# Expert tokens in 32 chunks of 64 rows on both column halves of the PE array, instead of 24 chunks of 128 rows

## The reference, cut to what matters

```
x (544, 1024) = the normed rows
group  = argmax of x @ w_rg (4 groups); 2 best of the 4 experts in that group by x @ w_re
gate   = softmax over the two, times the group's probability
hid    = silu(x @ w1[e]) * (x @ w3[e])        w1, w3: 16 experts of (1024, 256)
y     += gate * hid @ w2[e]                   w2:     16 experts of (256, 1024)
```

## Time and profile before

| | |
|---|---|
| median of 3 runs | 1552.7 us (1549.16 to 1556.25) |
| the profiled execution's own time | 1555.62 us |
| its span in the profile | 1553.6 us |
| mean granted TensorE clock | 0.902 of full speed |
| TensorE matmul busy | 82% of the span |
| bytes moved by DMA | 304 MB, mean 196 GB/s |

### The profile page before, as it was taken

The page is one execution under the profiler, slowest core; times in us unless marked ns, Lnnn a source line. Parts: engine busy times, 40 slices in busy tenths (PEclk is TensorE's granted clock), DMA queues, the critical chain, the costliest instruction groups (busy, mean ns, idle before and its releaser), DMA issues.

```text
span 1553.6 us, 20055 instructions
## 1 busy us (share of the span) xinstructions
PE 1268.4 (82%) x6991; PEld 828.4 (53%) x6991; DVE 451.1 (29%) x1106; ACT 296.7 (19%) x613; POOL 160.9 (10%) x229
## 2 busy tenths in 40 slices
PE   3699999656699999957888888874995799999990
PEld 2377776433477777744555555553644444444440
DVE  4200000654212223223444443433445111111116
ACT  2200001322122122112222222211210111111112
POOL 0000000400111112200000000000000121111110
PEclk9899999777799999977898898877997799999995
DMA  8733332259522221079887888657001999999934
GB/s 309 263 108 110 111 108 100 81 180 332 187 81 63 88 77 56 12 271 313 281 274 251 266 286 291 234 199 259 26 31 36 336 334 318 309 313 331 312 122 172
DMA packets 152741, 304.23 MB, mean 196 GB/s; under 512 B 16014, under 2 KB 79271, under 8 KB 150176
## 3 DMA queue, kind: packets, MB, share of 16 engines
q1 hardware_dynamic: 143264, 281.55, 53.9%
q0 software_dynamic: 9408, 21.82, 3.8%
HBM read 283.37 MB, written 50.00 MB: 215 GB/s over the span
## 4 chain that ended last, share of the span: by engine, by line
PE 75%; DVE 10%; issue 4%; DMA 4%; SPq 4%; ACT 2%; another core or an unknown queue 1%; POOL 0%; DVEq 0%; POOLq 0%; ACTq 0%
PE psum L841 64%; PE psum L1124 6%; DVE arena L1720 3%; DMA wring<-in_w_mod 2%; PE psum L1163 2%; PE psum L1388 1%; DVE wring L1728 1%; SPq L628 1%; DVE hT L2300 1%; PE psum L1052 1%; PE psum L970 1%; DVE wring L1720 1%; DVE arena L1728 1%; DVE xT L2091 1%
## 5 line engine op out<-in xcount | busy, mean ns | idle before, releaser
L841 PE MATMUL psum<-hT,wring 128*128 128x272 f32 x1280 | 303.9, 396 | 8.3 <-ACT hT L1445 8.3
L841 PEld LDWEIGHTS psum<-hT,wring 128*128 128x128 f32 x1280 | 241.2, 191 | 68.8 <-issue 20.8
L841 PE MATMUL psum<-arena 128*8 128x128 f32 (+6 forms) x1488 | 207.6, 338 | 6.6 <-DVE arena L1720 3.5
L841 PE MATMUL psum<-wring,hT 128*128 128x512 f32 x384 | 173.0, 604 | 17.5 <-DVE hT L2300 15.4
L841 PEld LDWEIGHTS psum<-arena 128*8 128x8 f32 (+5 forms) x1488 | 109.9, 119 | 92.7 <-issue 78.3
L841 PE MATMUL psum<-wring,arena 128*8 128x128 f32 (+3 forms) x1008 | 118.2, 411 | 19.6 <-DMA wring<-in_w_mod 14.0
L841 PEld LDWEIGHTS psum<-wring,hT 128*128 128x128 f32 x384 | 71.8, 192 | 104.8 <-issue 101.8
L841 PEld LDWEIGHTS psum<-wring,arena 128*8 128x8 f32 (+3 forms) x1008 | 51.9, 111 | 74.2 <-issue 60.4
L841 PE MATMUL psum<-arena,small 128*128 128x256 f32 (+8 forms) x162 | 51.5, 442 | 39.7 <-DVE arena L1720 27.7
L1124 PE MATMUL psum<-small,arena 128*128 128x128 f32 x392 | 65.3, 322 | 20.8 <-DMA arena<-in_cache_kv 13.1
L779 POOL TENSOR_SCALAR wring<-wring,arena 128x384 f32<-128x384 f32 (+6 forms) x32 | 45.7, 1427 | 292.0 <-DVE arena L1939 292.0
(11 more groups left out here) (236 smaller groups left out, 1207.7 us busy)
## 6 DMA issues: line engine op xcount, KB each, us to landing
wring<-in_w SPq DMA_DIRECT2D x48, 1024.0 KB, 11.2
arena<-in_cache_kv SPq DMA_DIRECT2D x128, 320.0 KB, 3.5
wring<-in_w_mod SPq DMA_DIRECT2D x12, 2048.0 KB, 13.4
arena<-in_w SPq DMA_DIRECT2D x24, 1024.0 KB, 5.0
xT<-in_cache_kv SPq DMA_DIRECT2D x64, 320.0 KB, 3.5
wring<-in_cache_kv SPq DMA_DIRECT2D x64, 320.0 KB, 3.6
out_dil_sample<-in_cache_dil SPq DMA_DIRECT2D x8, 2044.0 KB, 37.0
wring<-in_w_in SPq DMA_DIRECT2D x6, 2048.0 KB, 11.8
```

The lines of the kernel that those rows point to most:

```text
L841: return T.matmul(out, lhsT, rhs, start=start, stop=stop, **k)
```

## The change

```
-CHUNKS = NEXP + (TOP * TOK - NEXP) // P
+CROWS = 64
+OVER = 16
+CHUNKS = NEXP + OVER
+WSLOTS = 4
...
+        OVER_AT = [n // 2 if n % 2 == 0 else OVER - 1 - n // 2 for n in range(OVER)]
...
+            def base_weights(e):
+                slot = 2 * e % WSLOTS
+                if e >= 2:
+                    sp.wait_ge(sem("h_mm"), 2 * (e - 2) + 1)
+                for n, name in enumerate(("w1", "w3")):
+                    sp.dma_start(w13_at[slot][:, n, :], I[name][0, e].rearrange("(p k) f -> p (k f)", p=P)
+                                 ).then_inc(sem(f"ld_e{slot}"), 16)
+                if e >= 2:
+                    sp.wait_ge(sem("y_mm"), 2 * (e - 2) + 1)
+                sp.dma_start(w2_at[slot], I["w2"][0, e].rearrange("(k p) f -> p k f", p=P)
+                             ).then_inc(sem(f"ld_e{slot}"), 16)
+            sp.wait_ge(sem("gate_mm"), 3 * GATES)
+            base_weights(0)
...                                   (the stores of h_d, as before)
-            sp.wait_ge(*done_at("exp_id"))
...
+            for e in range(1, NEXP):
+                base_weights(e)
...
             def scatter(c):
-                pool.wait_ge(sem("yc_evA"), c + 1)
-                pool.wait_ge(sem("yc_evD"), c + 1)
+                pool.wait_ge(sem("yc_ev"), c + 1)
                 settle()
                 pool.indirect_dma_start(
-                    out=y_d, out_offset=bass.IndirectOffsetOnAxis(ap=row_i[:, c:c + 1], axis=0),
+                    out=y_d.rearrange("t (a d) -> (t a) d", a=2),
+                    out_offset=bass.IndirectOffsetOnAxis(ap=row_i[:, c:c + 1], axis=0),
...
+            def over_weights(c):
+                slot, j = c % WSLOTS, OVER_AT[c // 2]
+                if c >= WSLOTS:
+                    pool.wait_ge(sem("h_mm"), c - WSLOTS + 1)
+                    pool.wait_ge(sem("y_mm"), c - WSLOTS + 1)
+                    settle()
+                for n, name in enumerate(("w1", "w3")):
+                    pool.indirect_dma_start(out=w13_at[slot][:, n, :], ...
+                for n in range(2):
+                    pool.indirect_dma_start(out=w2_at[slot][:, n, :], ...
             settle()
-            for c in range(CHUNKS + RING):
-                if c < CHUNKS:
-                    gather(c)
-                if c >= RING:
-                    scatter(c - RING)
+            for c in range(RING):
+                gather(c)
+            over_weights(1)
+            over_weights(3)
+            for c in range(CHUNKS):
+                scatter(c)
+                if c + RING < CHUNKS:
+                    gather(c + RING)
+                if c % 2 and c + WSLOTS < CHUNKS:
+                    over_weights(c + WSLOTS)
...
+            def turn_rows(c):                                  # TensorE
+                pe.wait_ge(sem(f"ld_g{c % RING}"), 16 * (c // RING + 1))
+                if c >= 2:
+                    pe.wait_ge(sem("xg_ev"), c - 1)
                 for k in range(KD):
+                    last = T.transpose(banks[c % 2][:, CROWS * k:CROWS * k + CROWS],
+                                       xrow[0:CROWS, c % RING, 128 * k:128 * k + 128], ident[0:CROWS, 0:CROWS])
+            def hidden(c):
...
                 for k in range(KD):
+                    for side in range(2):
+                        f0 = DE * k + P * side
+                        last = mm(banks[2 + c % 2][CROWS * side:CROWS * side + CROWS, 0:256],
+                                  xg[:, c % RING, CROWS * k:CROWS * k + CROWS], w13_at[slot][:, :, f0:f0 + P], ...
+            def outputs(c):
+                pe.wait_ge(sem("hidT_ev"), c + 1)
+                if c >= 2:
+                    pe.wait_ge(sem("yc_ev"), c - 1)
                 for k in range(2):
+                    for side in range(2):
+                        last = mm(banks[5 + c % 2][CROWS * side:CROWS * side + CROWS, :],
+                                  hidT[:, c % RING, CROWS * k:CROWS * k + CROWS],
+                                  w2_at[c % WSLOTS][:, k, 512 * side:512 * side + 512], ...
+            turn_rows(0)
+            turn_rows(1)
+            for c in range(CHUNKS):
+                hidden(c)
+                if c:
+                    outputs(c - 1)
+                if c + 2 < CHUNKS:
+                    turn_rows(c + 2)
+                turn_hidden(c)
+            outputs(CHUNKS - 1)
...
+            def outputs_out(c):                                # VectorE
+                dve.wait_ge(sem("y_mm"), c + 1)
+                if c >= RING:
+                    dve.wait_ge(sem(f"st_yc{c % RING}"), 16 * (c // RING))
+                V.tensor_copy(ychunk[:, c % RING, :], banks[5 + c % 2]).then_inc(sem("yc_ev"), 1)
```

More of the change, by code:

```diff
@@ L643, in _ @@
             sp.wait_ge(sem("row_t"), 5)
-            sp.wait_ge(*done_at("exp_id"))
[L646 to L671, removed]
+            for e in range(1, NEXP):
+                base_weights(e)
             for s in range(RING):
-                sp.wait_ge(sem(f"st_yc{s}"), 16 * (CHUNKS // RING))
+                sp.wait_ge(sem(f"st_yc{s}"), 16 * len(range(s, CHUNKS, RING)))
             for i in range(5):
@@ L1401, in turn_hidden @@
-            def turn_hidden(i, c0, slot):
-                pe.wait_ge(sem("hid_ready"), i * RING + (c0 + 1))
-                if c0:
-                    pe.wait_ge(sem("hidT_ev"), i * RING + c0)
-                for k in range(2):
-                    last = T.transpose(banks[5][:, 128 * k:128 * k + 128], hidr[:, slot, 128 * k:128 * k + 128], ident)
-                last.then_inc(sem("hid_t"), 1)
-            def outputs(i, c0, slot, before=True):
-                pe.wait_ge(sem("hidT_ev"), i * RING + (c0 + 1))
-                pe.wait_ge(sem(f"ld_e{slot}"), i * 16 + 16 * (c0 // RING + 1))
-                for half in range(2):
-                    if before:
-                        pe.wait_ge(sem("yc_evD" if half else "yc_evA"), i * RING + c0)
-                    for k in range(2):
-                        last = mm(banks[6 + half], hidT[:, slot, 128 * k:128 * k + 128],
-                                  wdown[:, slot, 1024 * k + 512 * half:1024 * k + 512 * half + 512], k == 0, k == 1)
-                    last.then_inc(sem("y_mm"), 1)
@@ L1421, in _ @@
-            turn_rows(0, 0, 0)
-            hidden(0, 0, 0)
-            turn_rows(0, 1, 1)
-            turn_hidden(0, 0, 0)
-            with pe.Fori(0, CHUNKS // RING - 1) as i:
-                for c0 in range(1, 1 + RING):
-                    hidden(i, c0, c0 % RING)
-                    outputs(i, c0 - 1, (c0 - 1) % RING, True)
-                    turn_rows(i, c0 + 1, (c0 + 1) % RING)
-                    turn_hidden(i, c0, c0 % RING)
-            for c in (CHUNKS - 2, CHUNKS - 1):
-                hidden(0, c, c % RING)
-                outputs(0, c - 1, (c - 1) % RING)
-                if c < CHUNKS - 1:
-                    turn_rows(0, c + 1, (c + 1) % RING)
-                turn_hidden(0, c, c % RING)
@@ new lines, in gate_half, with hidden_out @@
+            def gate_half(c):
+                act.wait_ge(sem("h_mm"), c + 1)
+                if c >= RING:
+                    act.wait_ge(sem("hid_ready"), c - RING + 1)
+                f(sil[:, c % RING, :], banks[2 + c % 2][:, 0:P], ACT.Silu).then_inc(sem("sil_ready"), 1)
+            def hidden_out(c):
+                act.wait_ge(sem("hid_t"), c + 1)
+                if c >= RING:
+                    act.wait_ge(sem("y_mm"), c - RING + 1)
+                A.copy(hidT[:, c % RING, :], banks[4][:, 0:P]).then_inc(sem("hidT_ev"), 1)
@@ L1710, in _ @@
+            features_out(0)
+            features_out(1)
+            for c in range(CHUNKS):
+                gate_half(c)
+                if c + 2 < CHUNKS:
+                    features_out(c + 2)
+                hidden_out(c)
             A.preload_act_table_set("natural_log_exp_and_others")
@@ new lines, in _ @@
+            link(tt(r_p1, r_p1, r_q, ALU.add))
+            link(ts(r_p2, r_p1, -4.0, 67.0, ALU.mult, ALU.add))
+            link(ts(r_p1, r_p1, 4.0, -3.0, ALU.mult, ALU.add))
+            link(tt(r_p1, r_p1, r_p2, ALU.min))
+            link(stt(r_ch, r_ch, 2.0, r_p1, ALU.mult, ALU.subtract))
+            link(stt(r_ch, r_q, 1.0, r_ch, ALU.is_lt, ALU.mult))
+            link(tt(r_ch, r_ch, r_p1, ALU.add))
+            for side in range(2):
+                tt(slot_oh[:, :, CROWS * side:CROWS * side + CROWS],
+                   row_ids[:, 0:CROWS].unsqueeze(1).to_broadcast([P, 10, CROWS]),
+                   r_s.unsqueeze(2).to_broadcast([P, 10, CROWS]), ALU.is_equal)
@@ L2331, in last_rows @@
+            for c in range(CHUNKS):
+                gated(c)
+                if c:
+                    outputs_out(c - 1)
+            outputs_out(CHUNKS - 1)
             def last_rows(i):
```

210 lines of the change are left out of this document (90 added, 120 removed).

## The result

| | before | after |
|---|---|---|
| median | 1554.01 us (4 runs, 1549.16 to 1556.25) | 1745.89 us (4 runs, 1743.71 to 1750.51) |
| ratio to before | | 1.124, 95% interval 1.121 to 1.128 |
| profiled execution's own time, span | 1555.62, 1553.6 us | 1750.51, 1748.8 us |
| mean granted TensorE clock | 0.902 | 0.833 |

The change costs 192 us; forecast were 1774 us and a range of 1690 to 1890. The span grew by 195.2 us, and the expert stage alone by 194.4: its first hidden product starts at 1216.43 and its last output product ends at 1709.31, 492.9 us where before it was 298.5.

A forecast was written before the change was run, and what follows sets the result against it. TensorE was taken as the bound before the change. Start at 1223.3, 8.5 for iteration 0, 29 x 17.0 = 493 and 13.5 end the outputs at 1738.3, +221 us: 1774 us, range 1690 to 1890.

The forecast's parts named there:

- The added wait: Ahead of row transposes in iterations 1 to 29, TensorE idles for a gather issued behind the scatter: 7.8 us (5.5 to 11.9).
- The clock: Behind each gap TensorE restarts at the low clock, adding 2.7 us to 6.5 us of work: 9.2 us an iteration.
- TensorE's work in a chunk: Expert stage, 64 rows at full clock with column halves side by side: 6.5 us.
- The period: One expert-stage iteration, 9.2 us of work plus 7.8 of gap: 17.0 us (12.0 to 24.9).
- Weights hidden: Expert stage: weight traffic under 210 GB/s and POOL's four extra indirect DMAs, some 5.2 us, cost nothing.
- What lies ahead of the stage: Before hidden(0): routing +3.1 us, one more set of row transposes +1.5, reordered reads 0; hidden(0) starts at 1223.3.
- Gather in time: Rival: the gather is in time after all and DMA bounds the expert stage, -55 us, 1498 us; chance 0.08.
- Halves in turn: Rival: column halves take turns on top of the gap, 22.3 us an iteration, +154, 1928 us; chance 0.06.
- Clock never back: Rival: the clock stays low throughout the expert stage, 20.8 us an iteration, +110, 1884 us; chance 0.12.
- clock hardly falls: Rival: the clock hardly falls with the gap in place, 14.3 us an iteration, -78, 1696 us; chance 0.06.
- Gather behind weights: Rival: the gather queues behind weights and lands at 8.5 us, 21.1 an iteration, +119, 1893 us; chance 0.06.
- the three rivals outside the range: Rivals at 1498, 1928 and 1893 us, outside 1690 to 1890; the forecast said the range leaves out some 0.18.

The follow-up runs named there:

- The filled gap: Changed kernel plus six products of 512 columns that serve nothing, between outputs and row transposes in iterations 1 to 29: 1712.2 us, ratio 1.104.
- the weights in order: Kernel with gather(c+5) ahead of scatter(c), plus SP's plain loads of an even chunk waiting until the preceding overflow weights landed: 1529.5 us, ratio 0.985.
- the gather first: Changed kernel with POOL issuing gather(c+3) ahead of scatter(c) instead of behind it: 1656.8 us, ratio 1.067.
- the gathers further ahead: Changed kernel with gather(c+5) ahead of scatter(c), two more gathers issued ahead of the loop: 1545.4 us, ratio 0.9965.

## Why the prediction was right, step by step

**The added wait, 7.8 us.** Right in place, count and size. It is in 29 iterations, ahead of the row transposes, released by the gather, 7.3 us each. Its first part was forecast at 3.43 from the outputs' end to the gather's issue and measured 3.28 (1410.51 to 1413.79). The landing was 4.4 in the sum, with bounds of 2.1 and 8.5, and measured 3.6 to 4.4, median 3.8: 0.6 too much, 17 us of the sum over 29 iterations. The estimate by the Trainium skill (DMA: Bandwidth & Descriptors, Anatomy of one DMA), 2.6 us for 256 KB, was 1.2 below the median of these gathers, and 1.0 below the fastest; the measurement decides, and taking the row was the better choice. Two gathers moved ahead bring the time back to that of before. That makes it shown.

**The clock, +2.7.** Forecast 9.2 us busy per iteration, measured 8.8, with 6.2 at the full clock: the slow part costs 2.6. The filled gap shows it from the other side. The rise back to the full level is within the iteration: hidden takes 4.7 to 6.4 us behind a gap, 3.67 without one, and outputs are at the full clock again (1.88).

**TensorE's work in a chunk, 6.5.** Measured 6.22 when chunks follow each other. Hidden 3.67 (3.6), outputs 1.89 (1.8), row transposes 0.71 (0.9), hidden transpose 0.33 (0.2); the rows overlap by a few tenths at their ends. The row transposes went by the wrong neighbour: with 64 rows they cost about what 32 rows cost (0.68). Column halves run side by side, as taken from the quarters. Of the drain at each change of the tiling mode, which the Trainium skill states (TensorEngine Tiling, Tiling Modes, Key Properties), no cost shows: three such changes lie in each chunk, and its 6.22 us are no more than the 6.60 of its parts.

**The period, 17.0.** Measured 16.14: 0.5 us less of gap, 0.4 less of work. Over 29 iterations that is 25 us. For the profiled execution the forecast was 1776.7 and the time 1750.5, 26.2 less. The stage's start, 6.9 us early, has its part in that as well, and two things go the other way: iteration 0 and the last two took 3.1 us more than in the sum (the wait of 2.8 us below, and hidden(30), which still stands behind a gap), and what follows the stage, taken as unchanged, grew by 2.8 (3.1 by the spans). In it POOL issues the last scatter 3.6 us after its tiny product, where the others take 0.8; the profile shows nothing that it waits for. These 5.9 us hide as much of the errors above; to that extent the total is closer than its terms, by luck.

**Weights hidden.** Right for this kernel, and now shown: without the overflow's bytes the period is the same. POOL's four issues took 1.0 us each with 0.3 between, as forecast, behind the gather. One wait was missed, a single 2.8 us of hidden(1) for its weights. They landed by 1225.9, well before the 1232 that was forecast, but hidden(0) was done sooner still.

**What lies ahead of the stage.** The routing grew by 3.4 us on POOL's way to the first gather (24.27 to 27.63 us), 3.1 forecast. The extra row transposes (+1.5) cost nothing. They hide beside the copy of the first features: from the first transposes to hidden(0) it is 2.89 us, and was 2.86. The reordered addition was taken at 0 and costs 0.8 us each: on VectorE's timeline of the changed kernel, where before it was 1.23,

```profile
1136.64 2.03 DVE L1728 TENSOR_TENSOR wring<-wring,arena 128x1024 f32<-128x1024 f32 x1
```

about 1.2 us of it on the path, inside the bounds given. hidden(0) still came 6.9 us earlier than forecast, since the part that the change doesn't touch ran 6.3 us earlier in this execution (the products at 1110.38 now start at 1104.10), the extra transposes were hidden, and the first gather took 0.5 us less. The 6.3 us are no merit of the change or of the forecast.

**The rivals.** Gather in time (1498): that case was built and is at 1545, or 1529 with the weights in order. The mechanism was put rightly, DMA becomes the bound, but its price was too low. It took 370 to 388 GB/s from two short windows, and the loaded stage sustains 295 to 327. Halves in turn: excluded by the rows. Clock never back, clock hardly falls: excluded by 0.71 in the stage and the full-clock outputs in each iteration. Gather behind weights: not in the changed kernel (landing never above 4.4), but it is what the gather meets as soon as its order is mended, which the argument against it (period longer than the load) says and which I did not follow further. The chances of the three rivals outside the range sum to 0.20, not 0.18.

## What to carry to other kernels

Where a load's issue is put behind a step that waits for the result of the work just done, count how many iterations lie between that wait and the first use of the load: at none, the whole round trip (copy out, issue, landing, here 7.3 us) stands in each iteration, however little any engine is busy. Add to it what the engine's clock loses behind each stop, here another 2.6 us. And when such a wait is removed, ask at once which transfer is next in the same queue, and price the bandwidth bound from the longest loaded stretch of the trace, not from its best one.

## What the runs showed of the hardware that was not expected

- Useless work can pay: six products of 512 columns in each gap (5.4 us in all) raised the stage's granted clock from 0.71 to 0.96 and took 34 us off the total.
- Products on the two column halves overlap even where they belong to different groups with different column counts (hidden on one half, outputs on the other, rows at 1308.64 to 1309.28).
- An addition of 128x1024 whose elements are read and written in another order takes 2.0 us instead of 1.2.
- In the changed kernel a third less DMA traffic (179 to 119 GB/s) changed a gather's landing by 0.1 us (3.8 and 3.9, medians). With shorter periods the same gather took longer: median 7.3 and at most 11.9 us with the gather first, 9.7 and 20.5 with the gathers further ahead.
- Making SP wait before it loads made the kernel 16 us faster (1545.4 to 1529.5), 17 us in the stage (291.2 to 273.9).
